# Transformer stack in split fp32: one eight-slot weight ring shared by raw and low halves, and modulation units summed four to a bank and placed elsewhere

## What is computed

```python
def ada_modulation(cond, w, b):                      # w: 1024 x 6144, per layer
    m = jax.nn.silu(cond) @ w + b
    return jnp.split(m, 6, axis=-1)

sh1, sc1, g1, sh2, sc2, g2 = ada_modulation(c, w_ada[i], b_ada[i])
csh1, csc1, cg1, csh2, csc2, cg2 = ada_modulation(c_ctx, w_ada[i], b_ada[i])
h = modulate(x, norm_mix[i], sh1, sc1)               # rmsnorm * (1 + scale) + shift
x = x + g1[:, None, :] * o                           # o: GLA (layer 0) or MLA (layer 1)
x = x + g2[:, None, :] * conv_ffn(modulate(x, norm_ffn[i], sh2, sc2), w_up, conv_w, conv_b, w_down)

def conv_ffn(h, w_up, conv_w, conv_b, w_down):       # D_FF = 2816
    u = depthwise_conv3(h @ w_up, conv_w, conv_b)
    a, g = jnp.split(u, 2, axis=-1)
    return (jax.nn.silu(g) * a) @ w_down
```

## Time and profile before

| | |
|---|---|
| median of 3 runs | 1509.61 us (1508.39 to 1511.23) |
| the profiled execution | 1503.95 us, its span 1502.0 us |
| PE busy | 1415.6 us, 94% of the span |
| PEld, POOL, ACT, DVE busy | 77%, 47%, 46%, 40% |
| mean granted TensorE clock | 0.970 |
| moved by DMA | 210.01 MB, mean 140 GB/s |

### The profile page before, as it was taken

How to read it: one execution, slowest core, us unless ns; L and a number is a source line. 1 busy time by engine, 2 the same in 40 slices (tenths; PEclk the granted TensorE clock), 3 DMA queues, 4 the chain that set the end, 5 groups by cost and what they waited for, 6 DMA issues and landing times.

```text
span 1502.0 us, 23985 instructions
## 1 busy us (share of the span) xinstructions
PE 1415.6 (94%) x8348; PEld 1157.9 (77%) x8348; DVE 601.0 (40%) x1101; ACT 683.6 (46%) x1042; POOL 711.6 (47%) x307
## 2 busy tenths in 40 slices
PE   5899899988899999999998989899999998999998
PEld 1668676766677777778887734789999986899998
DVE  3411764543523333330005744354442276354410
ACT  2552322423434343342225943366665566566642
POOL 0433100333234333434443610368889776588886
PEclk9999999999999999999999978999999999999999
DMA  9423454123344545443332410155556552355563
GB/s 324 149 72 96 158 193 179 60 72 97 123 165 145 182 148 176 151 140 100 110 98 93 126 42 1 64 183 182 181 180 209 168 166 78 113 175 187 183 197 126
DMA packets 60057, 210.01 MB, mean 140 GB/s; under 512 B 6369, under 2 KB 9697, under 8 KB 59873
## 3 DMA queue, kind: packets, MB, share of 16 engines
q1 hardware_dynamic: 59568, 207.52, 42.0%
q10 hardware_dynamic: 432, 1.70, 0.3%
HBM read 208.15 MB, written 1.05 MB: 139 GB/s over the span
## 4 chain that ended last, share of the span: by engine, by line
PE 88%; DVE 3%; ACT 2%; DMA 2%; issue 2%; SPq 1%; POOL 1%; ACTq 0%; DVEq 0%; POOLq 0%
PE ps L271 67%; PE ps L348 3%; DMA raw<-wstream 2%; PE ps L855 2%; PE ps L1155 2%; PE ps L1154 1%; PE ps L313 1%; PE ps L314 1%; PE ps L364 1%; PE ps L849 1%; PE ps L841 1%; PE ps L305 1%; PE ps L1163 1%; POOL wlo L257 1%; PE ps L835 1%
## 5 line engine op out<-in xcount | busy, mean ns | idle before, releaser
L257 POOL TENSOR_TENSOR wlo<-raw,whi 128x1024 fp32r<-128x1024 f32 x291 | 699.3, 2414 | 767.4 <-ACT whi L251 767.4
L251 ACT ACTIVATE whi<-raw 128x1024 fp32r<-128x1024 f32 x291 | 306.7, 1054 | 262.0 <-PE ps L271 238.9
L271 PE MATMUL ps<-Hhi,whi 128*128 128x256 f32 (+1 forms) x1360 | 409.0, 325 | 1.3 <-DVE Hlo L1325 1.3
L271 PE MATMUL ps<-Hlo,whi 128*128 128x256 f32 (+1 forms) x1360 | 403.0, 321 | 0.0
L271 PEld LDWEIGHTS ps<-Hhi,whi 128*128 128x128 f32 x1360 | 259.8, 191 | 36.9 <-issue 15.2
L271 PEld LDWEIGHTS ps<-Hlo,whi 128*128 128x128 f32 x1360 | 259.8, 191 | 19.5 <-issue 1.7
L271 PE MATMUL ps<-Hhi,wlo 128*128 128x256 f32 (+1 forms) x1360 | 241.3, 320 | 0.0
L271 PEld LDWEIGHTS ps<-Hhi,wlo 128*128 128x128 f32 x1360 | 203.2, 191 | 18.4
L641 DVE SCALAR_TENSOR_TENSOR u<-ps,par,u 128x255 f32<-128x255 f32 (+1 forms) x132 | 75.4, 571 | 213.4 <-ACT u L601 212.9
L271 PE MATMUL ps<-hidhi,whi 128*128 128x256 f32 (+1 forms) x528 | 155.1, 319 | 0.0
L271 PE MATMUL ps<-hidlo,whi 128*128 128x256 f32 (+1 forms) x528 | 154.9, 319 | 0.0
(11 more groups left out here) (280 smaller groups left out, 1709.6 us busy)
## 6 DMA issues: line engine op xcount, KB each, us to landing
raw<-wstream SPq DMA_DIRECT2D x387, 512.0 KB, 3.5
XT<-x_t SPq DMA_DIRECT2D x1, 1024.0 KB, 10.0
XT<-ctx_t SPq DMA_DIRECT2D x1, 1024.0 KB, 12.1
memx<-mem_t ACTq DMA_DIRECT2D x1, 1024.0 KB, 5.3
out_t<-XT SPq DMA_DIRECT2D x1, 1024.0 KB, 5.2
par<-params SPq DMA_DIRECT2D x1, 457.5 KB, 3.4
glac<-gla_consts SPq DMA_DIRECT2D x1, 384.0 KB, 12.3
mlac<-mla_consts ACTq DMA_DIRECT2D x1, 320.0 KB, 3.4
```

The costliest lines, as they stand in the source:

```text
L251: nc.scalar.activation(whi[:, n % RING, :], raw[:, n % RING, :], ACT.Copy).then_inc(S["hi_ready"], 1)
L257: nc.gpsimd.tensor_tensor(wlo[:, n % RING, :], raw[:, n % RING, :], whi[:, n % RING, :].bitcast(F32), ALU.subtract).then_inc(raw_done[n % ...
L271: mm = nc.tensor.matmul(o, a, b, start=start, stop=stop)
```

## The change

`raw` and `wlo` become one ring of eight slots (the two tensors lie at the same addresses): POOL writes the low half over the raw weights. A load waits until PE has used the slot eight places earlier (`slot_used`, counted in the order `TAKEN` in which PE takes the slots), for split and modulation slots alike. Four units are summed into one PSUM bank: `cs` gets 38 columns, and a window that moves by two places each unit's two rows, so there are 6 instead of 24 `mod_row`, `mod_turn` and `mod_bias`. The units stand in other places. Loops over four tiles become loops over eight, and the loops over `go`, `mo` and the down slots are written out.

```diff
+RAWS = 8
...
+QUEUE = [unit(0, 0), unit(0, 1), unit(0, 2), ("gate", "gate", 0, 1), ("gq", "gq", 0, 1), unit(0, 3), ("gq_", "gq", 1, 3)] + whole("gk", "gv")
+QUEUE += [unit(0, u) for u in range(4, 12)] + whole("gr") + [unit(1, 0), unit(1, 1)] + whole("gr_b") + [unit(1, 2)] + whole("go") + [unit(1, 3)]
+QUEUE += whole("up0", *[f"up0_{_i}" for _i in range(10)])
...
+DN0_UNITS = {5: 4, 8: 5, 11: 6, 14: 7, 17: 8, 19: 9, 21: 10}
+for _j in range(24):
+    QUEUE += [(f"dn0_{_j}" if _j else "dn0", "dn0", _j, 1)] + ([unit(1, DN0_UNITS[_j])] if _j in DN0_UNITS else [])
+QUEUE += [unit(1, 11)] + whole("cq", "ckv", "kpe", "uq", "uk", "uv", "mo", "up1", "dn1")
...
+TAKEN = list(range(NSLOTS))
+for _early, _unit in (("gate", "mod0_3"), ("gr", "mod1_0")):
+    _before = range(RAW[_early], RAW[_unit])
+    for _rank, _slot in enumerate([RAW[_unit] + _s for _s in range(MOD_UNIT)] + list(_before)):
+        TAKEN[_slot] = RAW[_early] + _rank
+
+
+def used(n):
+
+    return TAKEN[RAW_OF[n]] + 1
...
-        raw = sb(ctx, "raw", [P, RING, 1024])
+        with ExitStack() as same:
+            raw = sb(same, "raw", [P, RAWS, 1024])
+        wlo = sb(ctx, "wlo", [P, RAWS, 1024], F32R)
...
         def load_slot(sp, n, turns=0):
+            if n >= RAWS:
+                sp.wait_ge(S["slot_used"], TAKEN[n - RAWS] + 1 + RAWS * turns)
+            sp.dma_start(raw[:, n % RAWS, :], wstream[turns * RAWS + SRC[n]]).then_inc(raw_in[n % RAWS], 16)
+        def hi_slot(act, n, i=0):
+            r = RAW_OF[n]
+            act.wait_ge(raw_in[r % RAWS], 16 * (r // RAWS + 1) + 16 * i)
             if n >= RING:
-                sp.wait_ge(raw_done[n % RING], turns + n // RING)
-            sp.dma_start(raw[:, n % RING, :], wstream[turns * RING + SRC[n]]).then_inc(raw_in[n % RING], 16)
-        def hi_slot(act, n, it=0, turns=0):
-            r = RAW_OF[n]
-            act.wait_ge(raw_in[r % RING], 16 * (r // RING + 1) + 16 * turns)
-            if n >= RING:
-                act.wait_ge(S["slot_used"], n - RING + 1 + it)
-            nc.scalar.activation(whi[:, n % RING, :], raw[:, n % RING, :], ACT.Copy).then_inc(S["hi_ready"], 1)
-        def lo_slot(pool, n, it=0):
-            pool.wait_ge(S["hi_ready"], n + 1 + it)
-            if n >= RING:
-                pool.wait_ge(S["slot_used"], n - RING + 1 + it)
-            nc.gpsimd.tensor_tensor(wlo[:, n % RING, :], raw[:, n % RING, :], whi[:, n % RING, :].bitcast(F32),
-                                    ALU.subtract).then_inc(raw_done[n % RING], 1)
-        def slot_products(pe, n, it, turns, hi_products, lo_products, signal=None):
-            pe.wait_ge(S["hi_ready"], n + 1 + it)
-            for source, products in ((whi, hi_products), (wlo, lo_products)):
-                if source is wlo:
-                    pe.wait_ge(raw_done[n % RING], RAW_OF[n] // RING + 1 + turns)
+                act.wait_ge(S["slot_used"], used(n - RING) + RAWS * i)
+            nc.scalar.activation(whi[:, n % RING, :], raw[:, r % RAWS, :], ACT.Copy).then_inc(S["hi_ready"], 1)
+        def lo_slot(pool, n, i=0):
+            pool.wait_ge(S["hi_ready"], n + 1 + RAWS * i)
+            r = RAW_OF[n] % RAWS
+            nc.gpsimd.tensor_tensor(wlo[:, r, :], raw[:, r, :], whi[:, n % RING, :].bitcast(F32), ALU.subtract).then_inc(S["lo_ready"], 1)
+        def slot_products(pe, n, i, hi_products, lo_products, signal=None):
+            pe.wait_ge(S["hi_ready"], n + 1 + RAWS * i)
+            for source, products in ((whi[:, n % RING], hi_products), (wlo[:, RAW_OF[n] % RAWS], lo_products)):
+                if products is lo_products:
+                    pe.wait_ge(S["lo_ready"], n + 1 + RAWS * i)
                 for o, c0, width, stationary, other, start, stop in products:
-                    w = source[:, n % RING, c0:c0 + width]
+                    w = source[:, c0:c0 + width]
                     a, b = (w, other) if stationary else (other, w)
                     mm = nc.tensor.matmul(o, a, b, start=start, stop=stop)
             mm.then_inc(signal or S["slot_used"], 1)
...
-        def mod_products(pe, n, turns, bank):
+        MOD_BANK = {0: 2, 1: 7, 2: 7, 3: 7, 4: 3, 5: 2}
+        def mod_products(pe, layer, u):
+            n, v, batch = RAW[f"mod{layer}_{u}"], u % 4, 3 * layer + u // 4
+            if v == 0 and batch in (2, 3):
+                pe.wait_ge(S["mod_out"], batch)
             for s in range(MOD_UNIT):
-                pe.wait_ge(raw_in[(n + s) % RING], 16 * ((n + s) // RING + 1) + 16 * turns)
+                r = n + s
+                pe.wait_ge(raw_in[r % RAWS], 16 * (r // RAWS + 1))
                 for k in (2 * s, 2 * s + 1):
                     g = k % 4
-                    mm = nc.tensor.matmul(ps[32 * g:32 * g + 32, bank, :], cs[:, k, :], raw[:, (n + s) % RING, 512 * (k % 2):512 * (k % 2) + 512],
-                                          start=k < 4, stop=k >= 4)
-                mm.then_inc(raw_done[(n + s) % RING], 1)
-        def mod_row(act, n, turns, u, bank):
-            last = n + MOD_UNIT - 1
-            act.wait_ge(raw_done[last % RING], last // RING + 1 + turns)
-            if not isinstance(u, int) or u >= 1:
-                act.wait_ge(S["mod_tr"], u)
-            nc.scalar.activation(modrow[:, :], ps[:, bank, :], ACT.Copy).then_inc(S["mod_row"], 1)
-        def mod_turn(pe, u, bank):
-            pe.wait_ge(S["mod_row"], u + 1)
+                    mm = nc.tensor.matmul(ps[32 * g:32 * g + 32, MOD_BANK[batch], :], cs[:, k, 6 - 2 * v:38 - 2 * v],
+                                          raw[:, r % RAWS, 512 * (k % 2):512 * (k % 2) + 512], start=v == 0 and k < 4, stop=v == 3 and k >= 4)
+                mm.then_inc(S["slot_used"], 1)
+        def mod_row(act, batch):
+            act.wait_ge(S["slot_used"], TAKEN[RAW[f"mod{batch // 3}_{batch % 3 * 4 + 3}"] + MOD_UNIT - 1] + 1)
+            if batch >= 1:
+                act.wait_ge(S["mod_tr"], batch)
+            nc.scalar.activation(modrow[:, :], ps[:, MOD_BANK[batch], :], ACT.Copy).then_inc(S["mod_row"], 1)
+        def mod_turn(pe, batch):
+            pe.wait_ge(S["mod_row"], batch + 1)
             for j in range(4):
-                mm = nc.tensor.matmul(ps[:, bank, 2 * j:2 * j + 2], modrow[:, j * P:(j + 1) * P],
-                                      con[:, CCOL["sel"]:CCOL["sel"] + 2], start=True, stop=True)
+                mm = nc.tensor.matmul(ps[:, MOD_BANK[batch], 8 * j:8 * j + 8], modrow[:, j * P:(j + 1) * P], sel[:, :], start=True, stop=True)
             mm.then_inc(S["mod_tr"], 1)
...
             for u in range(4):
                 if u == 3:
                     norm_pe(pe, "mix0", TT)
-                if u >= 2:
-                    pe.wait_ge(S["mod_row"], u - 1)
-                mod_products(pe, RAW["mod_a"] + MOD_UNIT * u, 0, u % 2)
-                if u >= 1:
-                    mod_turn(pe, u - 1, 2 + u - 1)
-            mod_turn(pe, 3, 5)
+                mod_products(pe, 0, u)
+            mod_turn(pe, 0)
...
-            for u in range(4):
-                mod_row(act, RAW["mod_a"] + MOD_UNIT * u, 0, u, u % 2)
-                if u == 2:
-                    norm_root(act, "mix0", TT)
-            for n in range(RING):
-                hi_slot(act, n)
+            norm_root(act, "mix0", TT)
+            hi_slot(act, 0)
+            hi_slot(act, 1)
+            mod_row(act, 0)
+            hi_slot(act, 2)
...
-            def four_tiles(i):
-                for j in range(4):
-                    pe.wait_ge(S[f"{t}_free"], i * 4 + j + 1)
-                    if isinstance(i, int) and j < firsts:
-                        if j == firsts - 1:
-                            first_tiles(pe, s0, range(firsts), xhi, xlo, ntok, norm)
-                    else:
-                        column_tile(pe, s0 + j, j, xhi, xlo, ntok, i * 4, i * (2 if f == 0 else 1))
-                    if f == 0 and j == (firsts - 1 if isinstance(i, int) else 0):
-                        pe.wait_ge(S["mod_row"], i + 13)
-                        mod_products(pe, RAW["mod_c0"], i * 2, 4)
-                if f == 0:
-                    pe.wait_ge(S["mod_out"], i + 13)
-                    mod_turn(pe, i + 13, 5)
-            four_tiles(0)
-            with pe.Fori(1, FF_T // 2) as i:
-                four_tiles(i)
+            def up_tile(j, i):
+                pe.wait_ge(S[f"{t}_free"], i * 8 + j + 1)
+                column_tile(pe, s0 + j, j % 4, xhi, xlo, ntok, i)
+            for j in range(firsts):
+                pe.wait_ge(S[f"{t}_free"], j + 1)
+            first_tiles(pe, s0, range(firsts), xhi, xlo, ntok, norm)
+            if f == 0:
+                mod_turn(pe, 3)
+            for j in range(firsts, 4):
+                up_tile(j, 0)
+            with pe.Fori(0, 5) as i:
+                for j in range(4, 12):
+                    up_tile(j, i)
             d0 = START[f"dn{f}"]
...
-            def down(m, i):
-                pe.wait_ge(S[f"{t}_dn"], i * 4 + m + 1)
-                if f == 0 and m == 1:
```

(68 more changed lines are left out.)

279 lines of the change are left out of this document (147 added, 132 removed).

## The result

The changed kernel takes 1468.5 us (median of 4 runs, 1467.1 to 1474.0), the kernel before beside it 1510.2 (1508.4 to 1511.2). The ratio is 0.973, with a 95% interval from 0.971 to 0.976. The forecast was 1477, with a range from 1467 to 1489. The profiled execution has a span of 1465.3 us, against 1502.0.

The account below looks back on a forecast made before the run. The prediction took PE's work plus 86 us of PE waiting as the bound. Its terms summed to -32.8 us, taken from 1509.61 to give 1477, with a range of 1467.5 to 1489.

Parts of the forecast that it names:

- f0, up tiles: f0's up stage: without units it takes one turn and 41 tiles of 5.53 us, -46.2 us.
- f0, down slots: f0's down stage: seven units return at 1.92 us each in full, plus 0.84 for a turn, +14.3 us.
- `gr`: Behind the fourth `gr` tile: PE waits for a late load, ACT's high half and `sr`; +6.5 us, bounds 1.9 and 8.
- the clock's term: Lower granted clock: half of an earlier loss kept, plus 1.5 us for the new stall in `gr`, +2.4 us.
- GLA loop and around: Earlier scores -1.2 us, shorter loop -8.6, sums behind the loop -1.9.
- Norms: Norms ffn0 and mix1: logarithm waits behind ACT's last high half, +1.3 us each, 0.84 for a turn; +3.4 together.
- Head: Before the first tile: early first halves against two more slots to load, -1.5 us, between -4 and +1.5.
- Costs of nothing: Units 4, 5, 2, 3, 11 and most of 0 hidden under other work; 1.92 us each if cover is missing.
- Jumps do not stall: Rival, up loops: 12 jumps back each stall for an instruction fetch, 42 us, total 1519; chance 0.04.
- Units in the down slots: Rival, f0's down stage: units cost what they cost in the up loop, +6 us, total 1483; chance 0.12.
- ACT and DVE do not hold the up tiles: Rival denied here, f0's up loop: ACT and DVE hold tiles, 0.3 us each, +12, total 1489; chance 0.04.
- The stall in `gr`: Rival said no stall behind the fourth `gr` tile: 4.6 of the 6.5 us go, total 1472; chance 0.10.

Follow-up runs that it names:

- e_up4: e_row with units (1,4) to (1,7) and their turn back in f0's up stage, written out there instead of looped: 1469.4 us, ratio 0.974.
- e_dbl_dense: e_row with the products of the seven units between f0's down slots, (1,4) to (1,10), issued twice: 1472.7 us, ratio 0.976.
- e_row: The changed kernel with ACT making the row of batch 4 before, not behind, the high half of down slot 20: 1460.8 us, ratio 0.970.
- e_gr: The changed kernel with unit (1,1) moved from behind the fourth `gr` tile to behind the sixth: 1472.5 us, ratio 0.977.
- e_best: The changed kernel with the edits of e_row and e_gr, and ACT's last high half behind the logarithm in norms ffn0 and mix1: 1460.4 us, ratio 0.968.
- e_dbl_cover: e_row with the products of units (0,4), (0,5), (1,2), (1,3) and (1,11) issued twice, same transfers: 1460.2 us, ratio 0.971.
- e_pad: e_row with an unused tensor of 992 bytes a partition ahead of modrow, restoring earlier SBUF addresses behind it: 1466.4 us, ratio 0.973.
- e_ring4: e_row with the eight-slot ring used only four deep from f0's fifth slot on: 1548.6 us, ratio 1.026.

## Why the forecast came out right, and where it did not

**f0, up tiles (-46.2, measured -50.0).** The mechanism is right and the size of a tile was off. I took 16.59/3 = 5.53 from the earlier trace rows; that row stands behind a unit and holds the restart. A tile is 24 x 0.2267 = 5.44 before and after. Eleven units with 0.27 of restart and ten turns with 0.12 are 4.2 us that I had left in the tiles; e_up4 shows 0.26 by itself.

**f0, down slots (+14.3, measured +25.4).** This is the step that failed: "so it is 1.92: 7 x 1.92 + 0.84 for a turn". The units do cost 1.85 each (e_dbl_dense), 0.13 of restart behind them, and the turn its 1 us; but the turn waits, 7.9 us and 2.7 of clock. I had counted out the ring for `gr`, found the high half in front of an ACT operation that PE needs, and did not do the same for the row of batch 4, which stands behind the high half of down slot 20, whose place in the ring was unit (1,8)'s. e_row takes away all of it by moving one line. Without it this term would have been +14.8.

**`gr` (+6.5, measured +7.7).** Place, releasers and size as forecast: the load behind the fourth tile, ACT, `sr`, then the tile; a gap of 6.5 us with the unit in it. The tail was 3.3 instead of 5.0, and 2.7 us of lower clock came behind the gap, for which the clock's term had 1.5. e_gr shows that the wait follows the distance in the ring.

**GLA loop and around (-11.7, measured -14.7).** Passes are 10.31 us instead of 10.7: the unit takes 1.85 and nothing waits. The clock loss of which I kept half did not come in this execution; in e_row's it did, 1.5 us at the first sums. So part of this is chance.

**`go` (0, measured -2.1).** The kernel before had lost some 2 us to the lower clock in that stretch (mean granted clock 0.95, 1.00 in the changed kernel), which was not part of my reading.

**Norms (+3.4, measured +1.9, with first tiles).** The logarithm is 4.5 us behind the last tile, 4.8 forecast and 3.5 before, so +1.0 and not +1.3; e_best takes that back at ffn0. The rest goes with a higher granted clock in ffn0 (0.93, 0.87 before).

**Head (-1.5, measured -1.1).** Right within what one execution shows.

**Costs of nothing.** The five covered units are covered (e_dbl_cover). "Everything later (mla to f2) has the same instructions" holds for PE's products and was still 4 us off: it had left out that the change moves tensors. `cs` went out of the common part of SBUF, all that lies behind it moved by 992 bytes, and e_pad, with the tensors at the old places, takes 2.6 us more in f1 and 2.1 in f2.

**The rivals.** Jumps do not stall: 1116 matmuls stand in one piece over the jumps of a loop of 192. By the rule that I had quoted from the Trainium skill, page "Runtime: NRT & Kernel Launch", section "Instruction fetch mechanics", a stall at each jump was possible; this trace shows none. Units in the down slots do not cost 2.77. ACT and DVE do not hold the up tiles. The stall in `gr` is there. The head is 1.1 shorter and not longer.

**The sum.** The spans differ by 36.7 us, where the terms gave 32.8. Against one error of +11 in the down stage stand -4 in the up stage, -3 around the GLA loop, -4 behind mix1, -2 in `go` and -2 of clock. The medians differ by 41.7, since the profiled execution before lay 6.3 under its runs' median (1510.2) and the one after 1.4. That the total was nearer than its parts is luck: with the one wait taken out, e_row's 1460.8 us lie below the forecast range of 1467 to 1489.

## What to carry to other kernels

When loads, conversions and small vector copies share a ring and an engine's queue, list for each operation that the bound engine waits for what stands ahead of it in its own queue, and for that its place in the ring; do it at every such operation, not only at the first that is found. A slot that is freed at its last use and not at its conversion needs a deeper ring: e_ring4 shows it for one such ring, but how deep is enough was not tried. Take the cost of a tile from a long piece without interruptions, and read the restart behind an interruption as a cost of the interruption.
